# Stick-breaking attention of a decoder step: score, decay and sum stages reordered, sums taken with split operands

## What is computed

```python
mask = k_pos[None, :] < q_pos[:, None]
z = jnp.einsum('bqhd,bkhd->bhqk', qb, kb).astype(jnp.float32) * scale + bias
log_1m = jnp.where(mask, jax.nn.log_sigmoid(-z), 0.0)
log_w = jax.nn.log_sigmoid(z) + lax.cumsum(log_1m, axis=3, reverse=True) - log_1m
w = jnp.where(mask, jnp.exp(log_w), 0.0)
outs.append(jnp.einsum('bhqk,bkhd->bqhd', w.astype(vb.dtype), vb))
```

## Time and profile before

| | us |
|---|---|
| median of 3 runs | 2429.96 |
| the profiled execution | 2428.46 |
| its span, first to last instruction | 2426.8 |
| PE busy in the span | 2382.4 (98%) |
| DVE busy | 1241.0 (51%) |
| ACT busy | 994.5 (41%) |
| unit 27's last product to the first product of evout | 561.70 to 654.19 |

### The profile page before, as it was taken

The page is one execution under the profiler, slowest core; times in us unless marked ns, Lnnn a source line. Parts: engine busy times, 40 slices in busy tenths (PEclk is TensorE's granted clock), DMA queues, the critical chain, the costliest instruction groups (busy, mean ns, idle before and its releaser), DMA issues.

```text
span 2426.8 us, 43808 instructions
## 1 busy us (share of the span) xinstructions
PE 2382.4 (98%) x18802; PEld 2183.8 (90%) x18802; DVE 1241.0 (51%) x1725; ACT 994.5 (41%) x1399; POOL 114.9 (5%) x232
## 2 busy tenths in 40 slices
PE   6999999999999999999999999999999999999998
PEld 5999999965699999999999999887777999999998
DVE  5533246755576333357523347755554758633245
ACT  5422235635456222346422245533223546522243
POOL 0000000122100000000000000012222100000000
PEclk9999999999999999999999999999999999999999
DMA  8555345785537653565754255544545456642254
GB/s 308 180 183 183 124 149 179 252 211 139 190 113 228 215 173 95 188 206 175 261 184 156 83 168 189 188 153 165 170 165 165 136 177 182 206 126 88 87 179 155
DMA packets 122660, 417.10 MB, mean 172 GB/s; under 512 B 23387, under 2 KB 27611, under 8 KB 122211
## 3 DMA queue, kind: packets, MB, share of 16 engines
q1 hardware_dynamic: 88962, 301.92, 39.1%
q10 hardware_dynamic: 18144, 62.03, 7.1%
q0 software_dynamic: 15360, 50.34, 6.3%
HBM read 390.84 MB, written 23.41 MB: 171 GB/s over the span
## 4 chain that ended last, share of the span: by engine, by line
PE 88%; DVE 5%; ACT 3%; DMA 2%; issue 1%; SPq 0%; ACTq 0%; POOL 0%; DVEq 0%; POOLq 0%
PE PS L2026 70%; PE PS L1425 3%; PE PS L1960 2%; DVE WL L2318 2%; PE PS L1990 2%; PE PS L1355 1%; ACT WH L2140 1%; DMA AFIRST<-in_w_ada 1%; PE PS L791 1%; PE PS L1309 1%; PE PS L1340 1%; PE PS L1350 1%; PE PS L753 1%; DMA RAW<-in_w_out 1%; PE PS L1321 1%
## 5 line engine op out<-in xcount | busy, mean ns | idle before, releaser
L2318 DVE TENSOR_TENSOR WL<-RAW,WH 128x1024 fp32r<-128x1024 f32 (+1 forms) x478 | 633.0, 1325 | 647.9 <-ACT WH L2140 647.2
L2026 PE MATMUL PS<-HH,WH 128*128 128x260 f32 x3432 | 796.6, 285 | 3.2 <-DVE QKVS L1119 1.8
L2026 PE MATMUL PS<-HH,WL 128*128 128x260 f32 x3432 | 786.5, 283 | 0.0
L2026 PE MATMUL PS<-HL,WH 128*128 128x260 f32 x3368 | 769.6, 283 | 0.0
L2140 ACT ACTIVATE WH<-RAW 128x1024 fp32r<-128x1024 f32 (+1 forms) x478 | 542.2, 1135 | 425.4 <-PE PS L2026 267.0
L2026 PEld LDWEIGHTS PS<-HH,WH 128*128 128x128 f32 x3432 | 569.9, 188 | 25.4 <-issue 16.8
L2026 PEld LDWEIGHTS PS<-HH,WL 128*128 128x128 f32 x3432 | 569.4, 188 | 0.0
L2026 PEld LDWEIGHTS PS<-HL,WH 128*128 128x128 f32 x3368 | 557.0, 188 | 0.6 <-issue 0.2
L2026 PE MATMUL PS<-GH,WH 128*128 128x260 f32 x1408 | 386.4, 285 | 0.9 <-DVE WL L2318 0.8
L2026 PE MATMUL PS<-GL,WH 128*128 128x260 f32 x1408 | 384.2, 283 | 0.0
L2026 PE MATMUL PS<-GH,WL 128*128 128x260 f32 x1408 | 383.5, 283 | 0.0
(11 more groups left out here) (340 smaller groups left out, 2317.5 us busy)
## 6 DMA issues: line engine op xcount, KB each, us to landing
RAW<-in_w_in SPq DMA_DIRECT2D x236, 512.0 KB, 3.7
RAW<-in_w_out SPq DMA_DIRECT2D x120, 704.0 KB, 4.0
AW<-in_w_ada ACTq DMA_DIRECT2D x114, 512.0 KB, 5.5
RAW<-in_w_odd SPq DMA_DIRECT2D x60, 512.0 KB, 3.7
RAW<-in_w_odout SPq DMA_DIRECT2D x30, 512.0 KB, 3.9
RAW<-in_w_even SPq DMA_DIRECT2D x28, 512.0 KB, 4.0
KV<-in_v_pages POOLq DMA_DIRECT2D x32, 256.0 KB, 4.8
SR<-in_ret_past POOLq DMA_DIRECT2D x32, 256.0 KB, 4.0
```

The costliest lines, as they stand in the source:

```text
L2026: last = nc.tensor.matmul(ps[:, x, 0:HT], w[:, k * P:(k + 1) * P], src[k0 + k][:, x, :], start=(begin and t == 0), stop=(end and t == 2))
L2318: nc.vector.tensor_tensor(low_, RAW[:, from_:from_ + w], high_.bitcast(F32), ALU.subtract).then_inc(lo_done, 1)
```

## The change

What it does, part by part:

- **Sums in two fp32r passes.** ACT makes a rounded copy of each head's softplus (`high_part`, tiles SHA and SHB), DVE the remainder in place (`low_part`, SAL and others), and each product with TRI or ONES becomes two fp32r products with the copies TRIR and ONESR.
- **Order.** The scores of heads 0 and 1 (`first_scores`) now all stand inside value units 25 to 27, and so does the cumulative sum of the past (`sums_past`). The scores of pair 1 are interleaved with the sums of head 0. In turn t the scores of pair t+2 stand behind the sums of pair t. The absolute value is taken on DVE for all eight heads.
- **Homes.** ZB now lies where the pooling input UP was, and SHA and SHB behind it; so DVE's first bias of head 1 and ACT's first `high_part` wait for the four writes (`pool_out`), which therefore are issued before the load of output unit 0 and no longer before that of unit 3.

```diff
 def even_sp:
             for i in range(len(STEPS["evout"])):
-                if i == 3:
+                if i == 0:
                     sp.wait_ge(ev_act, EV_FULL)
                     sp.wait_ge(ev_dve, EV_FULL)
                     for dst, src in ((k_t[:, 0:4 * SEQ], KP[:]), ... (pool_n, US[:, :, :, 1:16])):
-                        sp.dma_start(dst, src).then_inc(out_done, 16)
+                        sp.dma_start(dst, src).then_inc(pool_out, 16)
+                if i == 3:
                     sp.wait_ge(vp_evac, 4)
 def even_pe:
-                pe.wait_ge(sp_done, h + 1)
+                pe.wait_ge(spl_done, h + 1)
...
+                for j in range(i, 4):
+                    w = TRIR if j == i else ONESR
+                    for x, part in enumerate((SPH[h % 2], SPL[h])):
+                        last = nc.tensor.matmul(PS[1][:, i % 2, (j - i) * P:LEN[i]], w[:],
+                                                part[:, OFF[j]:OFF[j] + LEN[j]], start=(j == i and x == 0),
+                                                stop=(j == 3 and x == 1))
...
+            for j in range(4):
+                scores(1, j)
+                sums(0, j)
             ada_step("start", 0)
             for t in range(PAIRS):
-                scores(t + 1, 0)
-                sums(2 * t, 0)
-                scores(t + 1, 1)
                 if t:
-                    values(t - 1)
-                sums(2 * t, 1)
-                scores(t + 1, 2)
-                sums(2 * t, 2)
...
+                    for i in range(4):
+                        sums(2 * t, i)
+                values_past(t)
                 ada_step("head", 2 * t)
                 for i in range(4):
                     sums(2 * t + 1, i)
...
+                scores(t + 2, 0)
+                scores(t + 2, 1)
+                if t < 3:
+                    values(t)
+                scores(t + 2, 2)
+                scores(t + 2, 3)
                 ada_step("head", 2 * t + 1)
 def even_act:
+            def high_part(h):
+                act.wait_ge(sp_done, h + 1)
+                if h == 0:
+                    act.wait_ge(pool_out, 64)
+                after(act, s_done, 4 * (h - 2) + 4)
+                nc.scalar.activation(SPH[h % 2], SP[h], ACT.Copy).then_inc(sph_done, 1)
...
+                if t < 3:
+                    decay(2 * t + 2)
+                    decay(2 * t + 3)
+                    table(LOG_SET)
+                    log(2 * t + 2)
+                    log(2 * t + 3)
+                    table(EXP_SET)
                 if t:
                     outputs(t - 1)
+                    weights(2 * t)
+                weights(2 * t + 1)
...
+                    high_part(2 * t + 2)
+                    high_part(2 * t + 3)
 def even_dve:
+            def low_part(h):
+                dve.wait_ge(sph_done, h + 1)
+                nc.vector.tensor_tensor(SPL[h], SP[h], SPH[h % 2].bitcast(F32), ALU.subtract).then_inc(spl_done, 1)
...
+                if t:
+                    low_part(2 * t)
+                    for i in range(4):
+                        log_weights(2 * t, i)
+                    low_part(2 * t + 1)
...
+                for i in range(4):
+                    log_weights(2 * t + 1, i)
...
+                softplus(2 * t + 2)
+                softplus(2 * t + 3)
...
+                for j in range(4):
+                    scored(t + 2, j)
+                sized(2 * t + 4)
+                sized(2 * t + 5)
```

More of the change, by code:

```diff
@@ L476, in decoder_step @@
         TRI = at("TRI", [P], g); g += size([P])
+        OS = at("OS", [4, NS], g); g += size([4, NS])
+        PSC = at("PSC", [4], g); g += 64
+        PT = at("PT", [NS * PAGES], g, I32); g += size([32])
         up_at = g
@@ L745, in values_unit @@
                 for tt in range(4):
-                    if tt == 2:
-                        side(i, 0)
-                        if j == 0:
-                            pe.wait_ge(ev_dve, EV_FULL)
+                    if tt:
+                        side(i, tt)
+                    if tt == 2 and j == 0:
+                        pe.wait_ge(ev_dve, EV_FULL)
                     for kk in range(2):
@@ L770, in even_pe @@
                 else:
-                    side(i, 1)
-            def scores_of_one():
-                for j in range(4):
-                    pe.wait_ge(vp_evac, 2) if j < 2 else pe.wait_ge(z_dve, 3 + j)
-                    score(1, j, PS[0][:, j % 2, 0:LEN[j]]).then_inc(z_done, 1)
+                    side(i, 4)
             def scores(t, j):
-                if t == PAIRS:
+                if t >= PAIRS:
                     return
-                pe.wait_ge(z_dve, biased_to(t, j))
+                if t == 1 and j == 0:
+                    pe.wait_ge(vp_evac, 2)
+                else:
+                    pe.wait_ge(z_dve, 8 * t + 2 * j)
                 for e in range(2):
@@ L925, in even_act @@
                     pooled(3)
[L926 to L941 removed]
+                if i == 26:
+                    table(EXP_SET)
+                    act.wait_ge(kv_used, 4)
+                    act.wait_ge(ident_ok, 4)
+                    for dst, src in ((TRIR, TRI), (ONESR, ONES)):
+                        nc.scalar.activation(dst[:], src[:], ACT.Copy).then_inc(const_ok, 1)
+                    act.wait_ge(zn_dve, 2)
+                    nc.scalar.activation(ZN[:, 1, :], ZN[:, 0, :], ACT.Abs).then_inc(zn_act, 1)
+                    act.wait_ge(zn_act, 1)
+                    nc.scalar.activation(ZN[:, 1, :], ZN[:, 1, :], ACT.Exp, scale=-1.0).then_inc(zn_act, 1)
+                    pooled_samples()
+                    decay(0)
+                    table(LOG_SET)
+                    act.wait_ge(zn_act, 2)
+                    nc.scalar.activation(ZN[:, 1, :], ZN[:, 1, :], ACT.Ln, bias=ONES[:, 0:1]).then_inc(zn_act, 1)
+                    log(0)
+            high_part(0)
+            table(EXP_SET)
+            value_rows(0)
             decay(1)
+            for tt in (1, 2, 3):
+                value_rows(tt)
             act.wait_ge(zn_dve, 4)
@@ L947, in even_act @@
             table(EXP_SET)
+            high_part(1)
             def outputs(t):
@@ L970, in even_act @@
             table(ROOT_SET)
-            act.wait_ge(out_done, 96)
+            act.wait_ge(pool_out, 64)
+            act.wait_ge(out_done, 32)
             for q, (n, hs) in enumerate(STEPS["evout"]):
@@ L1188, in even_dve @@
-                log_weights(2 * t, 2)
-                log_weights(2 * t, 3)
-                sized(t + 1, 1)
-                if t == 0:
-                    softplus(1)
-                ada_evac("head", 2 * t)
-                for i in range(2):
-                    log_weights(2 * t + 1, i)
-                if t < 3:
-                    softplus(2 * t + 2)
-                for i in range(2, 4):
-                    log_weights(2 * t + 1, i)
-                if t < 3:
-                    softplus(2 * t + 3)
+                for j in range(4):
+                    scored(t + 2, j)
@@ L1943, in _ @@
                 sp.dma_start(y_t[:, g:g + n, HT * x:HT * x + HT], X[:, g:g + n, x, :]).then_inc(y_out, 16)
[L1945 removed]
+            sp.wait_ge(pool_out, 64)
+            sp.wait_ge(out_done, 32)
             sp.wait_ge(rp_out, 32 * RH)
```

249 lines of the change are left out of this document (118 added, 131 removed).

## The result

The changed kernel takes **2470.25 us** (median of 4 runs, 2466.01 to 2477.64), the kernel before 2430.77 beside it (4 runs): a ratio of 1.0166, interval 1.0132 to 1.0199. It is slower, as forecast, but by 40 us instead of 22, and 3 us above the range. The profiled execution took 2466.01 us, with a span of 2464.4; before it was 2426.8, so 37.6 us have to be found. It is the fastest of the four. Its mean granted clock over the whole span is 0.989; in the slowest it is 0.984.

A forecast was written before the change was run, and what follows sets the result against it. PE was taken as the bound, busy 87.1 of 93 us in the changed stage. 2428.5 + 8.5 (turns) + 10 (pages) + 3.5 (clock) = 2450.5 us, median 1.5 above: 2452 us, range 2435 to 2467.

The forecast's parts named there:

- (1): Sign: PE waits at 528 before the third scores_past for 8 to 12 us; under 1 would mean pages in time.
- (4): Sign: PE's waits in the turns between the sums of heads 2, 4 and 6 are for DVE's low part and bias.
- (2): Sign: the sums of a head take 2.8 to 3.2 us from first to last start, less waits.
- (3): Sign: sums of head 4 start about 27 us after head 2's, head 6's 16 later; first under 20 disproves the walk.
- the walk: Instruction-by-instruction count of the new order from unit 26 to evout's start; it gave +8.2 us, taken as +8.5.
- the clock: Term for PE products at the lower clock after the page wait and the turns' waits: +3.5 us, bounds 0 and 8.
- two such: Clock drops counted in the sum: two stretches of 3.5 us at the lower level, each losing 1.7 us.
- The page wait: PE waits in scores_past for past-key pages held up by the early writes: +10 us, bounds 0 and 14.
- The first rival: The pages of past keys come in time despite the early writes: 2441 us, chance 0.20.
- The turns: New order of scores, sums and values up to evout costs +8.5 us, bounds +4 and +14.
- The saving: Split sums save PE 1.9 us for each head, 15 us for eight; forecast not to come through.
- PE stays the bound: Rival placed at DVE's low part in turn 1: the 15 us come through, 2416 us, chance 0.09.

The follow-up runs named there:

- e8: The changed kernel with its four writes late again, plus idle plain fp32 products in four of PE's waits; 2450.4 us, ratio 1.0072.
- e13: The kernel before, with only softplus written in fp32r and the sums taken in one pass, remainder left out; 2432.45 us, ratio 1.0013.
- e7: e2 with DVE's low part ahead of the score blocks, PE alternating scores and sums, and even-head weights moved along; 2449.8 us, ratio 1.0086.
- e12: e2 with only DVE's low part of head 2t+2 moved ahead of the score blocks; 2450.0 us, ratio 1.0090.
- e2: The changed kernel with the four writes put back ahead of the load of output unit 3; 2452.5 us, ratio 1.0089.
- e4: e2 with plain fp32 sums and no high and low parts, new order kept; 2447.35 us, ratio 1.0070.
- e16: e5 with ACT's weights of head 2t put back behind both ln; 2439.1 us, ratio 1.0049.
- e14: e13 with five idle plain fp32 products in a turn on PE; 2429.6 us, ratio 1.0001.
- e11: e5 with idle plain fp32 products ahead of the sums of heads 1 to 7; 2435.75 us, ratio 1.0022.
- e5: The kernel before, old order and late writes, all sums split in two fp32r passes, ACT's weights of head 2t ahead of ln; 2438.55 us, ratio 1.0043.
- e10: e6 with idle plain fp32 products on PE, 4.3 us in a turn; 2434.2 us, ratio 1.0016.
- e6: e5 with one fp32r pass for each block and no high or low part, remainder left out; 2433.1 us, ratio 1.0017.
- e3: The changed kernel without the write of pool_n, the other three writes staying early; 2453.5 us, ratio 1.0096.

## Why the prediction was right and wrong

**What held.** The direction, and most of the reasons. (1) PE waits at 527 before the third `scores_past`, (4) in the turns it waits for the low part (4.28 and 5.32; forecast 4.3 for the first) and for bias, (2) the sums of head 1 at full clock take 3.1 us from first to last start, in the 2.8 to 3.2 forecast; measured as the 4.79 were, to the next work of PE, they take 3.3, so a head saves 1.5 us and not 1.9, 12 us in all and not 15. (3) The distance from head 2 to head 4 was to be 27 us, from head 4 to head 6 16 us. The changed kernel has 31.9 and 19.6, but e8, where the clock is held, has 27.6 and 16.3. So for these two turns the walk was right at full clock, within 0.7 us in each.

**The term that failed: the clock**, +3.5 with bounds 0 and 8. The prediction counted "two such" drops of 1.7 us. The trace of after has the lower level on 30.6 us of the three turns from head 0 to head 6, and in the products behind the page wait. Behind that wait it cost 2.5 us (6.0 instead of 3.5), in the three turns 9.2 (e8 against the changed kernel, one execution of each): 11.7 in all. The error was the count. There were four waits of 4 to 5 us in my own walk and two drops in the sum, and in the rows only one example of a drop. In the trace of after each of the four (3.60, 4.28, 3.89 and 5.32 us) has 3.4 to 5 us of products at the lower level behind it: the mean clock is 0.54 from 611.5 to 615.2 us and 0.50 from 622.95 to 628.0, from 641.86 to 645.9 and from 654.81 to 659.6. So have two short waits, of 1.83 and 1.68 us, which the clock's term had left out (0.55 from 587.9 to 591.7, 0.57 from 669.4 to 673.4). The drops fall into sums and values that DVE and ACT are waiting for. It is not the length of the wait alone: in e8, where idle products filled the long waits before it, the clock stayed at 1.00 behind the same 1.68 us. The prediction cited the Trainium skill, TensorE: Matmul & The Clock Gate, Part 1, for the throttled level being the default and activity what releases it. The traces agree: the lower level is what PE has behind its waits, and e8 shows that idle products keep it away.

**The page wait**, +10 with bounds 0 and 14: 14.91. The bound itself was too low by 1: it let the stretch of narrow rows begin at 522 and the page land with its end, but the page issued at 523 took 18.7 us, as the longest of the earlier trace rows (18.5) had. I chose the middle where the row nearest in kind stood at the end. (The row of 4.6 us in the earlier trace rows is that of the pages issued from 519 to 522; those of 516 to 519 took 3.4. The one that counted, at 521.66, is among the former.) The first rival rested on the rule that each DMA engine takes packets from its queues in turn (the Trainium skill, DMA: Bandwidth & Descriptors, Queues, rings and completion order). In the four microseconds from 522 on 2130 packets of one queue pass and 10 of the other; whatever the turn is, it did not spare the pages. The measurement decides.

**The turns**, +8.5: at full clock this was right for two turns of four. The first part, to the end of the sums of head 1, came 1.8 us later than walked (605.9, less 14.1 and 2.5 for the page wait and the products behind it, against 587.5), and the last turn took 16.9 us at a clock of 1.00 instead of 15.5.

The three together: page +4.9, clock about +8 over its term, the rest of the turns about +2, which is the 15.5 us between 2450.5 and the profiled 2466.0. The median lies another 4.2 us above that execution, where 1.5 were allowed; the slower executions are those with the lower clock (0.984 to 0.987 against 0.989), so this too is most likely more of the clock.

**The saving.** The prediction said that the 15 us of PE do not come through because of the new order. That is only half of it: e13 shows that they do not come through in the old order either. "PE is the bound, since it is busy for 87 of 93 us" was read too simply; a second chain stood beside it. In a turn of about the same length 13.1 us pass on DVE and ACT alone. The prediction had this link in hand (ACT's `weights` gate the first bias of the next pair) and counted ACT by its busy time. The rival "PE stays the bound" did not win in two other placings of the low part either (e7, e12). Of the 22 us left in e2 the order is the larger part: with plain sums it costs 17 us (e4, 2447.35 against 2430.16), and the split sums cost 10 in the old order (e16, 2439.1 against 2429.3).

## What to carry to other kernels

- A busy share of 94% does not make an engine the only bound. Before its work is made cheaper, follow the chain of the others through one turn back to where it began (here bias, size, exp, table load, ln, table load, weights, bias of the next pair). The part of the turn in which nobody waits for the engine gives nothing back.
- In these traces idle time of PE is not free: each wait of 3.6 to 5.3 us had 3.4 to 5 us of products at the lower clock behind it, and two of under 2 us had as well. Count one drop for each such wait of the walk, and ask which products behind it somebody waits for.
- A write of 4096 rows of 60 bytes made page loads of 256 KB take up to 18.7 us; such a write belongs where no load is needed within 20 us, small as it is in KB.

## What was not expected of the hardware

- **Idle products can pay.** In e14 five plain fp32 products in a turn, read by nobody, made the kernel 2.8 us faster than e13 (2429.6 and 2432.45); in e11 3 us faster than e5; in e8 three turns 10.9 us shorter than in e2, of which 2 are left in the time. Not always: e10 is no faster than e6.
- **240 KB hold the DMA engines for some 15 us**: 34 GB/s in the microsecond shown, at a share of 173.8%: the packets' times overlap. A page of 256 KB issued then takes 18.7 us instead of 4.6.
- Left open: what the 3.77 us left in e3 are made of, and why the same wait of 1.68 us is followed by the lower clock in one kernel and not in the other.
